# The norm row of four feed-forwards and of the last norm: a matrix of ones and a power over 256 columns

## The reference, cut to what matters

```
def rms_norm_2(x, g):
    y = x * lax.rsqrt(jnp.mean(x * x, axis=-1, keepdims=True) + EPS)
    return y * g

def swiglu_ffn(h, w_in, w_out):
    g, u = jnp.split(h @ w_in, 2, axis=-1)
    return (jax.nn.silu(g) * u) @ w_out

x = x + 0.5 * swiglu_ffn(rms_norm_2(x, ffn_norm), w_in, w_out)    # six of these, F = 2816
...
return rms_norm_2(x, final_norm)
```

## Time and profile before

| what | value |
|---|---|
| median of three runs | 1907.14 us |
| the profiled execution, its own time | 1909.82 us |
| its span, first to last instruction | 1908.0 us |
| around the span | 1.82 us |
| mean granted clock of PE | 0.993 |
| busy PE, PEld | 98%, 91% of the span |
| busy DVE, ACT, POOL | 67%, 51%, 8% |
| chain that ended last, share of PE | 69% |
| weights moved | 324.78 MB, mean 170 GB/s |

### The profile page before, as it was taken

The page is one execution under the profiler, slowest core; times in us unless marked ns, Lnnn a source line. Parts: engine busy times, 40 slices in busy tenths (PEclk is TensorE's granted clock), DMA queues, the critical chain, the costliest instruction groups (busy, mean ns, idle before and its releaser), DMA issues.

```text
span 1908.0 us, 32413 instructions
## 1 busy us (share of the span) xinstructions
PE 1872.4 (98%) x13226; PEld 1729.0 (91%) x13226; DVE 1284.3 (67%) x1451; ACT 974.0 (51%) x1330; POOL 153.6 (8%) x163
## 2 busy tenths in 40 slices
PE   7999999999999999999999999999999999999998
PEld 6999999899999997899999999989999959998997
DVE  6666787777466666766785766676669686456665
ACT  5454565565454445444554544454445474455444
POOL 2020100131010003000120100010001001010000
PEclk9999999999999999999999999999999999999999
DMA  7555354435435554545443445545555404435553
GB/s 267 220 193 182 133 190 153 144 133 177 155 136 196 179 195 154 199 177 194 156 179 133 177 177 181 193 177 181 190 180 183 176 23 148 163 121 211 180 187 117
DMA packets 45988, 324.78 MB, mean 170 GB/s; under 512 B 5325, under 2 KB 5461, under 8 KB 7104
## 3 DMA queue, kind: packets, MB, share of 16 engines
q1 hardware_dynamic: 44640, 316.57, 46.2%
q0 software_dynamic: 1248, 6.77, 1.0%
HBM read 322.26 MB, written 1.06 MB: 169 GB/s over the span
## 4 chain that ended last, share of the span: by engine, by line
PE 69%; DVE 7%; POOL 2%; ACT 1%; issue 1%; POOLq 0%; DVEq 0%; ACTq 0%
PE PS L661 19%; PE PS L550 12%; PE PS L551 12%; PE PS L552 12%; PE PS L664 10%; DVE w_lo L2016 2%; DVE xT L2039 2%; PE PS L741 1%; PE PS L759 1%; POOL stat L475 1%; DVE x L2091 1%; POOL both L464 1%; PE PS L1272 0%; PE PS L1253 0%; PE PS L1292 0%
## 5 line engine op out<-in xcount | busy, mean ns | idle before, releaser
L2016 DVE TENSOR_TENSOR w_lo<-raw,w_hi 128x2048 fp32r<-128x2048 f32 x297 | 683.7, 2305 | 227.1 <-ACT w_hi L1339 226.8
L661 PE MATMUL PS<-xT,w_hi 128*128 128x512 f32 x2112 | 754.5, 401 | 12.3 <-DVE w_lo L2050 10.5
L1339 ACT ACTIVATE w_hi<-raw 128x2048 fp32r<-128x2048 f32 x298 | 569.2, 1911 | 289.5 <-PE PS L552 287.5
L664 PE MATMUL PS<-xT,w_lo 128*128 128x256 f32 x2112 | 594.4, 281 | 0.0
L661 PEld LDWEIGHTS PS<-xT,w_hi 128*128 128x128 f32 x2112 | 398.9, 189 | 109.1 <-DVE w_lo L2050 10.5
L664 PEld LDWEIGHTS PS<-xT,w_lo 128*128 128x128 f32 x2112 | 401.1, 190 | 0.2
L550 PE MATMUL PS<-h_hi,w_hi 128*128 128x256 f32 x1280 | 364.3, 285 | 0.5 <-DVE h_lo L2179 0.5
L551 PE MATMUL PS<-h_lo,w_hi 128*128 128x256 f32 x1280 | 362.1, 283 | 0.0
L552 PE MATMUL PS<-h_hi,w_lo 128*128 128x256 f32 x1280 | 362.0, 283 | 0.0
L550 PEld LDWEIGHTS PS<-h_hi,w_hi 128*128 128x128 f32 x1280 | 245.1, 191 | 5.0 <-DVE h_lo L2179 1.0
L551 PEld LDWEIGHTS PS<-h_lo,w_hi 128*128 128x128 f32 x1280 | 245.3, 192 | 0.2
(11 more groups left out here) (320 smaller groups left out, 2542.0 us busy)
## 6 DMA issues: line engine op xcount, KB each, us to landing
raw<-weights SPq DMA_DIRECT2D x298, 1024.0 KB, 4.8
arena<-mems POOLq DMA_DIRECT2D x5, 1024.0 KB, 5.9
x<-x_in SPq DMA_DIRECT2D x2, 512.0 KB, 5.9
raw<-weights SPq DMA_DIRECT2D x2, 512.0 KB, 7.4
out<-x SPq DMA_DIRECT2D x4, 256.0 KB, 2.9
both<-toep POOLq DMA_DIRECT2D x1, 512.0 KB, 4.0
arena<-toep POOLq DMA_DIRECT2D x1, 512.0 KB, 4.5
con<-consts SPq DMA_DIRECT2D x1, 498.0 KB, 12.1
```

What stands on the lines that cost most here:

```text
L661: pe.matmul(PS[:, bank + part, :], w_hi[:, slot, w:w + P], xT[:, k].rearrange("p a b -> p (a b)"), start=k == 0, stop=False, skip_group_ch ...
L664: last = pe.matmul(PS[:, bank + part, 0:S], w_lo[:, slot, w:w + P], xT_hi[:, k, :], start=False, stop=k == KC - 1, skip_group_check=True)
L1339: act.activation(w_hi[:, slot, :], raw[:, raw_slot, :], ACT.Copy).then_inc(hi_ready, 1)
L2016: dve.tensor_tensor(w_lo[:, slot, :], raw[:, raw_slot, :], w_hi[:, slot, :], ALU.subtract).then_inc(lo_ready, 1)
```

## The change

In the four feed-forwards that are neither the first nor the double one, and in the last norm, the row is made another way. PE multiplies the matrix of ones (128x128) with `acc` (128x256), which gives the sum of squares of every token on every partition. DVE turns that into mean plus EPS in `rrow`, 128x256. POOL raises `rrow` to the power -0.5 in place, over all 256 columns. The two sum matmuls, the two columns, the diagonal, the second matmul and ACT's copy of the row fall away there. DVE waits for POOL's power inside `plain_statistic`, before `up_sum`. The counters of the semaphores are corrected by the number of plain sites (`at.plain`) wherever another norm follows.

```diff
@@ POOL
-            def statistic(dst, double=False, chunks=KC):
+            def statistic(dst, double=False, chunks=KC, plain=False):
...
                 pool.wait_ge(var_ready, n + 1)
-                if not double:
+                if plain:
+                    pool.tensor_tensor(rrow[:], rrow[:], minus_half[:, 0:1].broadcast_to([P, S]), ALU.pow
+                                       ).then_inc(rcol_ready, 1)
+                elif not double:
                     pool.tensor_tensor(dst, var, minus_half[:, 0:2], ALU.pow).then_inc(rcol_ready, 1)
...
-                statistic(rcol, i == DOUBLE, 5 if i == 0 or stage == "finalnorm" else KC)
+                statistic(rcol, i == DOUBLE, 5 if i == 0 or stage == "finalnorm" else KC,
+                          stage == "finalnorm" or (stage == "ffn" and i not in (0, DOUBLE)))
@@ PE
+            def plain_row():
+
+                pe.wait_ge(acc_ready, at.stat + 1)
+                pe.matmul(PS[:, 1, 0:S], con[:, K_ONES:K_ONES + P], acc[:, 0, :], start=True, stop=True,
+                          skip_group_check=True).then_inc(sum_done, 1)
+                at.stat += 1
+                at.plain += 1
...
                 else:
-                    statistic_sums()
+                    plain_row()
                     paired(n0 + 1, (n0 + 1) % SPL, 6)
-                    statistic_row()
...
                     if first:
-                        pe.wait_ge(rrow_ready, at.stat)
+                        pe.wait_ge(var_ready, at.stat)
+                        pe.wait_ge(rrow_ready, at.stat - at.plain)
                     down(n + 2, (n0 + 4) % SPL, s, it * 2 + s, first, False)
...
                 if stage == "finalnorm":
-                    square_sums(4)
-                    statistic_row(bank=5)
+                    for c in (5, 6, None, 7):
...
+                        last = pe.matmul(PS[:, 5, 0:S], con[:, K_ONES:K_ONES + P], acc[:, 0, :] if c is None else sq[:, c, :],
+                                         start=c == 5, stop=c == 7, skip_group_check=True)
+                    last.then_inc(sum_done, 1)
@@ ACT
                     up_low(n0 + 2, 0)
-                    statistic_row(rrow)
+                    at.stat += 1
+                    at.plain += 1
                     silu(0, 0)
@@ DVE
+            def plain_statistic(bank, between=None):
+
+                dve.wait_ge(sum_done, at.stat + 1)
+                dve.tensor_scalar(rrow[:], PS[:, bank, 0:S], 1.0 / D, EPS, ALU.mult, ALU.add).then_inc(var_ready, 1)
+                at.stat += 1
+                at.plain += 1
+                if between is not None:
+                    between()
+                dve.wait_ge(rcol_ready, at.stat)
...
                     statistic(rcol, double)
+                    up_sum(0, 0)
+                    dve.wait_ge(rrow_ready, at.stat - at.plain)
                 else:
-                    statistic(rcol, between=next_split)
-                up_sum(0, 0)
-                dve.wait_ge(rrow_ready, at.stat)
+                    plain_statistic(1, next_split)
+                    up_sum(0, 0)
...
                 elif stage == "finalnorm":
-                    statistic(rcol, bank=4)
-                    dve.wait_ge(row_done, at.stat)
+                    plain_statistic(5)
                     for c in range(0, KC, 2):
                         dve.wait_ge(scaled, c + 2)
                         dve.tensor_tensor(x[:, c:c + 2, :], x[:, c:c + 2, :],
-                                          PS[:, 5, 0:S].unsqueeze(1).broadcast_to([P, 2, S]), ALU.mult).then_inc(normed, 1)
+                                          rrow[:].unsqueeze(1).broadcast_to([P, 2, S]), ALU.mult).then_inc(normed, 1)
```

More of the change, by code:

```diff
@@ L117, in __init__ @@
         self.stat = 0
+        self.plain = 0
         self.mem = 0
@@ L519, in _ @@
                     pool.wait_ge(tab_stored, 16)
-                    pool.wait_ge(rrow_ready, at.stat)
+                    pool.wait_ge(rrow_ready, at.stat - at.plain)
                     pool.dma_start(both[:], bass.AP(tensor=toep.tensor, offset=0, ap=[[1, P], [384, 4], [1, S]])
@@ L593, in statistic_row @@
             def statistic_row(double=False, bank=1):
-                pe.wait_ge(diag_ready, at.stat + 1)
+                pe.wait_ge(diag_ready, at.stat - at.plain + 1)
                 for j in range(2 if double else 1):
@@ L1327, in _ @@
                 if stage == "finalnorm":
-                    square_sums(4)
-                    statistic_row(bank=5)
+                    for c in (5, 6, None, 7):
+                        if c is None:
+                            pe.wait_ge(acc_ready, at.stat + 1)
+                        else:
+                            pe.wait_ge(sq_ready, KC * at.stat + c + 1)
+                        last = pe.matmul(PS[:, 5, 0:S], con[:, K_ONES:K_ONES + P], acc[:, 0, :] if c is None else sq[:, c, :],
+                                         start=c == 5, stop=c == 7, skip_group_check=True)
+                    last.then_inc(sum_done, 1)
         @block.scalar
@@ L1402, in statistic_row @@
             def statistic_row(dst, double=False, bank=1):
-                act.wait_ge(row_done, at.stat + 1)
+                act.wait_ge(row_done, at.stat - at.plain + 1)
                 if double:
```

## The result

The changed kernel takes 2093.81 us (median of four runs, 2092.45 to 2095.29) against 1907.75 us of the kernel before in the same comparison. The ratio is 1.0968, with a 95% interval of 1.0956 to 1.0981. The profiled execution has a span of 2093.5 us (before: 1908.0), 185.5 us more.

A forecast was written before the change was run, and what follows sets the result against it. PE, 98% busy, was taken to bound the kernel, except in the last norm's chain. Four feed-forwards (156.4) plus the last norm (40.4) add 196.8 us to 1907.1: 2104 us, own range 2095 to 2122 (chance 0.72), whole range 1960 to 2125.

The forecast's parts named there:

- the price of the power: POOL's power over 256 columns, called W: 0.71 us plus 254 columns at 0.165 us, 42.6 us (42.1 to 44.0).
- the clock term: Behind each plain feed-forward's new wait, PE's clock is at its lower level; tile n0+3 loses 2.7 us.
- step 4: Plain feed-forward: DVE's split holds POOL, so the power ends at split end + W - 0.14, 605.2 us.
- W - 6.2: Plain feed-forward: PE waits for up_sum behind the power (W long), so tile n0+3 starts 36.4 us later.
- Step 7: Plain feed-forward: the slow tile n0+3 hides late h_lo from the down tile; at full clock PE would wait 1.1 us.
- W - 2.2: Last norm: DVE's scaling starts later by the power's time W less 2.2 us, 40.4 us.
- The cheaper long operand: Rival: POOL's power costs a third per column, 0.055 us, W = 14.7, giving 1964 us; chance 0.15.
- The rival on the other side: Rival: the power's columns cost as little as an add's, W = 1.3, so not slower, 1903.5 us; chance 0.10.
- The rival on the order: Rival: POOL begins before the split and holds DVE; up_sum starts within 0.3 us of the same time, no other total.

The follow-up runs named there:

- the run with the filling: The changed kernel with 290 useless 128x256 matmuls put on PE ahead of its wait for up_taken in the four plain feed-forwards; 2090.26 us.
- the curve: The changed kernel with POOL raising only 16, 64, 128 and 192 columns in the four feed-forwards, 256 in the last norm; 2000.6 us in one run.
- the run with the product: The changed kernel with its power replaced by a product with 0.000001 over the same 256 columns at all five places; 1903.65 us.

## Why the prediction was right

The forecast was 2104 us in a range of 1960 to 2125; the result is 2093.8. The mechanism held in every step. The narrow range that went with it, 2095 to 2122, missed the result by 1.2 us: the price of the power and the clock term were both too high. By its steps:

- *The price of the power*, 42.6 us from two rows over 2 and 4 columns, is 41.13. The slope was 0.165 and is 0.159; an error of 0.006 us a column, carried over 254 columns and five places, is 7.3 of the 10.7 us by which the forecast is too high (196.8 us forecast, 186.1 between the medians). The interval that I drew, 42.1 to 44.0, did not hold it: two rows that lie two columns apart, each told to 0.01 us, can't bound a price so closely 252 columns further on, and it should have been wider.
- *POOL behind the split*: 43.12 us with it, 41.13 without, so the power's work does begin only as the split ends, as step 4 says.
- *up_sum and what is queued behind it.* Tile n0+3 starts 34.9 us later than before (604.28 against 569.57, the changed kernel being 0.19 us ahead there). With W - 6.2 at W = 41.1 it is 34.9.
- *The clock.* The first feed-forward pays 2.64 us, forecast 2.7. The mean of the four is 148.3 / 4 - 34.9 = 2.2, as the tiles themselves have it (8.18, 7.46, 7.10 and 8.37 us against 5.54), since the clock came back after six and five pairs in two of them. That is another 2.1 us of the surplus. The last 1.3 lie where the change does nothing, and in the difference between profiled executions and medians.
- *h_lo hidden by the slow tile*: in the changed kernel the down tile follows without a wait; in the run with the filling it waits. Step 7 is right in its order. Its size at full clock was 1.1 us, and the run with the filling shows 0.66 (6.20 - 5.54): h_lo is written 6.7 us after the start of `up_sum` and not 7.3, as ACT's table load of 1.28 us ahead of the silu, which stood behind the row before, now falls into the wait (both read in the first plain feed-forward). I had sized the experiment with the filling without this step.
- *The last norm*: W - 2.2 = 38.9, measured 39.0.
- *The rivals.* The cheaper long operand is refuted by the curve. The rival on the other side was sound in its structure, as the run with the product shows (1903.65, worked out 1903.5), and wrong only in the price of the operation; that the two figures agree so closely is partly luck, since the product takes 0.61 us and not the 1.3 of that sum, which makes the last norm 1.5 us shorter (6.32 against 7.83) and not 0.9. The rival on the order said that POOL could hold DVE with no other total. In the changed kernel the split was first; where the power is first, it doesn't hold DVE, and the total is 4.9 us less than the changed kernel's.

## What to carry to other kernels

Before an operation is widened, look for its own price per element, from two sizes of that same operation in the trace: a product over 256 columns costs 0.61 us on POOL here and a power 41.13, so the price of another operation would have misled. Work out the point at which the wider form becomes late for its user (here some 4.6 us, against 0.7 to 41), and ask what is queued behind the new wait. A form that makes the row from one matmul can pay a little if the root is taken on engines that have slack at that place, and the saving is then what PE no longer does, some 0.7 us a place (2.9 of 1907 us in all here), not the length of the chain that was removed.

## What the runs showed of the hardware that I had not expected

- POOL's power is close to linear over two decades of size: 0.70 to 0.72 us for 2 columns, 1.04 for 4, 2.89 for 16 (4.88 less the 1.99 of the split), 41.13 for 256, 0.159 us for each column of 128 partitions from 16 on.
- DVE's subtraction and POOL's power were held in one order only. A DVE subtraction of two SBUF operands that was running held POOL's power for 1.99 us (43.12 against 41.13), and a power that was running did not hold the same subtraction (2.28 us, in 41.14 us of power). Why is open; no run here takes it apart.
- DVE's reciprocal over 256 columns took 1.74 us, where its mean over 256 took 0.41.
